# Last attention of a two-block transformer kernel: score matmuls of two heads issued in turn, and a fourth buffer for the position biases

## The reference

```python
proj = h @ w_in                                   # q, k, v of 3 groups x 16 heads, and a gate z
for g, (window, dilation) in enumerate(((128, 1), (512, 4), (2048, 16))):
    q, k = rms_norm(q_g), rms_norm(k_g)           # per head of 64
    logits = q @ k.T * 64 ** -0.5 + bias[distance, head]   # only causal distances that are
                                                  # multiples of dilation, up to window
    out_g, lse_g = softmax(logits) @ v, logsumexp(logits)
o = sum_g softmax_over_groups(lse)_g * out_g      # the same as one softmax over all keys of all groups
x = x + (o * silu(z)) @ w_out
```

## Time and profile before

| | us |
|---|---|
| median of 3 runs | 2271.77 (2268.54 to 2274.81) |
| profiled execution, its own time | 2273.13 |
| span of the profiled execution | 2271.3 |
| mean granted PE clock over the span | 0.884 |
| busy: PE / PEld / DVE / ACT / POOL | 2038.2 / 1693.6 / 1237.4 / 911.3 / 74.3 |

### The profile page before, as it was taken

One profiled execution on the slowest core, in us unless ns is written; L12 is line 12 of the kernel. 1 busy time (PEld: TensorE's weight loads), 2 busy tenths in 40 slices (PEclk: granted clock), 3 DMA queues, 4 the chain that ended last, 5 costly groups with the idle time before them and its releaser, 6 DMA issues.

```text
span 2271.3 us, 27874 instructions
## 1 busy us (share of the span) xinstructions
PE 2038.2 (90%) x11307; PEld 1693.6 (75%) x11307; DVE 1237.4 (54%) x1928; ACT 911.3 (40%) x1213; POOL 74.3 (3%) x135
## 2 busy tenths in 40 slices
PE   5899878868999999989967789987999899999998
PEld 3678656546777777868835668966999698888887
DVE  3553365653655565554356557765666554555443
ACT  4434512232444443344352245544334355664221
POOL 0100000011000000010000100001000000000000
PEclk8899977769999999989957799998999999997557
DMA  7534100002345442224300045544666455545321
GB/s 260 176 127 159 61 1 1 1 1 93 127 154 160 153 149 80 97 90 147 130 19 1 1 158 186 186 157 122 188 188 188 153 151 174 176 163 121 40 31 37
DMA packets 211453, 261.41 MB, mean 115 GB/s; under 512 B 4657, under 2 KB 173283, under 8 KB 211071
## 3 DMA queue, kind: packets, MB, share of 16 engines
q1 hardware_dynamic: 207690, 248.34, 33.8%
q0 software_dynamic: 3232, 11.15, 3.0%
q10 hardware_dynamic: 405, 0.15, 0.0%
HBM read 258.50 MB, written 1.12 MB: 114 GB/s over the span
## 4 chain that ended last, share of the span: by engine, by line
PE 68%; issue 13%; DVE 10%; ACT 4%; DMA 4%; POOL 1%; SPq 0%; DVEq 0%; ACTq 0%; POOLq 0%
PE acc L625 16%; PE acc L626 15%; PE acc L627 15%; PE acc L1068 3%; PE acc L1091 3%; DVE scratch L1784 2%; PE acc L799 2%; PE acc L655 2%; PE acc L656 2%; PE acc L1080 2%; ACT weights_high L1230 1%; DVE weights_low L1618 1%; PE acc L844 1%; PE acc L1024 1%; PE acc L847 1%
## 5 line engine op out<-in xcount | busy, mean ns | idle before, releaser
L1618 DVE TENSOR_TENSOR weights_low<-weights,weights_high 128x2048 fp32r<-128x2048 f32 x232 | 526.6, 2273 | 586.5 <-ACT weights_high L1230 586.2
L1230 ACT ACTIVATE weights_high<-weights 128x2048 fp32r<-128x2048 f32 x232 | 439.9, 1899 | 609.2 <-DMA weights<-in_w_ada_dram 117.2
L625 PE MATMUL acc<-normed_t_high,weights_high 128*128 128x256 f32 (+1 forms) x1824 | 577.5, 317 | 4.8 <-DVE normed_t_low L1652 2.6
L626 PE MATMUL acc<-normed_t_low,weights_high 128*128 128x256 f32 (+1 forms) x1824 | 564.8, 310 | 0.0
L627 PE MATMUL acc<-normed_t_high,weights_low 128*128 128x256 f32 (+1 forms) x1824 | 563.4, 309 | 0.0
L625 PEld LDWEIGHTS acc<-normed_t_high,weights_high 128*128 128x128 f32 x1824 | 346.4, 190 | 36.6 <-DVE normed_t_low L1652 6.8
L626 PEld LDWEIGHTS acc<-normed_t_low,weights_high 128*128 128x128 f32 x1824 | 343.9, 189 | 22.7 <-issue 3.8
L627 PEld LDWEIGHTS acc<-normed_t_high,weights_low 128*128 128x128 f32 x1824 | 344.1, 189 | 20.7
L625 PE MATMUL acc<-weights_high,normed_t_high 128*128 128x512 f32 (+1 forms) x792 | 314.0, 397 | 28.5 <-DVE normed_t_low L1925 28.4
L626 PE MATMUL acc<-weights_low,normed_t_high 128*128 128x512 f32 (+1 forms) x792 | 310.3, 392 | 0.0
L627 PE MATMUL acc<-weights_high,normed_t_low 128*128 128x512 f32 (+1 forms) x792 | 310.0, 391 | 0.0
(11 more groups left out here) (216 smaller groups left out, 2238.7 us busy)
## 6 DMA issues: line engine op xcount, KB each, us to landing
weights<-in_w_ada_dram SPq DMA_DIRECT2D x48, 1024.0 KB, 5.2
weights<-in_w_up_dram SPq DMA_DIRECT2D x44, 1024.0 KB, 6.4
weights<-in_attn_w_in_dram SPq DMA_DIRECT2D x40, 1024.0 KB, 5.1
weights<-in_conv_w_in_dram SPq DMA_DIRECT2D x32, 1024.0 KB, 5.8
weights<-in_w_in_dram SPq DMA_DIRECT2D x24, 1024.0 KB, 6.3
weights<-in_w_down_dram SPq DMA_DIRECT2D x20, 1024.0 KB, 5.0
weights<-in_w_out_dram SPq DMA_DIRECT2D x8, 1024.0 KB, 5.1
weights<-in_conv_w_out_dram SPq DMA_DIRECT2D x8, 1024.0 KB, 5.0
```

The source lines that it names most:

```text
L625: pe.matmul(o, ah, bh, start=start, stop=False)
L626: pe.matmul(o, ah, bl, start=False, stop=False)
L1230: act.activation(hi_slot(n)[:, 0:used], slot(n)[:, 0:used], ACT.Copy).then_inc(hi_in.sem, 1)
L1618: dve.tensor_tensor(slot(n, ring_lo)[:, 0:used], slot(n)[:, 0:used], hi_slot(n)[:, 0:used], ALU.subtract).then_inc(lo_in.sem, 1)
```

## The change

The list of units is reordered so that two neighbouring heads form a pair: (0,0), (1,0), (0,1), (1,1), (2,0), ... PE issues scores only in even steps, for the two units st and st+1 (same t, heads 2i and 2i+1), matmul by matmul in turn: group 0 of the even head, group 0 of the odd head, and so on, first all of the two first banks, then the two second banks. Transposes and V products keep their places, one unit per step. VectorE and ScalarE run the same loops as before, over the new list. The biases get a fourth buffer, in the space of `ht_b` (which the low part of the split input uses until the last gate product): head h goes to buffer h modulo 4, from head 4 on it waits for the maximum of unit (h-4, 1), and head 3 waits for the last of the gate products `z2`.

```diff
--- before.py
+++ after.py
@@ -225,7 +225,9 @@
         cosT, sinT = part(wide, 256), part(wide, 256)
         m0 = at[0]
         SM = part(wide, 2304).rearrange("p (d l n) -> p d l n", d=2, l=9)
-        BIAS = wide[:, m0:m0 + 2304].rearrange("p (b g n) -> p b g n", b=3, g=NG)
+        bias_old = wide[:, m0:m0 + 2304].rearrange("p (b g n) -> p b g n", b=3, g=NG)
+        BIAS = [*(bias_old[:, b, :, :] for b in range(3)), ht_b[:, 0:768].rearrange("p (g n) -> p g n", g=NG)]
+        NBIAS = len(BIAS)
         MASK = masks[:, :].rearrange("p (d l n) -> p d l n", d=2, l=LEVELS)
         pos = [0]
 
@@ -298,7 +300,7 @@
         s_fw = sem("final_weight_in")
         s_vec = sem("bias_rows_out")
         s_hot = sem("hot_in")
-        s_bias = [sem(f"bias_in{i}") for i in range(3)]
+        s_bias = [sem(f"bias_in{i}") for i in range(NBIAS)]
         s_out = sem("result_out")
         vector_step, scalar_step, pool_step = sem("vector_step"), sem("scalar_step"), sem("pool_step")
 
@@ -369,7 +371,7 @@
         q_rs = S("qk_scale", QKEYS)
         q_done = S("qk_scaled", QKEYS)
         zk = [(c, t) for c in range(2) for t in range(2)]
-        BU = [(h, t) for h in range(NH) for t in range(2)]
+        BU = [(2 * i + j, t) for i in range(NH // 2) for t in range(2) for j in range(2)]
         b_max = S("b_max", BU)
         b_exp = S("b_exp", BU)
 
@@ -1058,16 +1060,19 @@
                         pe.wait_ge(*taken_after(("v2", g, c, t)))
             U = len(BU)
             for st in range(U + 3):
-                if st < U:
-                    h, t = BU[st]
-                    r = slice(64 * (h % 2), 64 * (h % 2) + 64)
+                if st < U and st % 2 == 0:
+                    t = BU[st][1]
                     n = (t + 1) * P
                     for part_, gs in enumerate(((0, 1), (2,))):
-                        o = open_group(("s2", st, part_))
+                        outs = [open_group(("s2", u, part_)) for u in (st, st + 1)]
                         for g in gs:
-                            last = pe.matmul(o[:, g % 2 * 256:g % 2 * 256 + n], QK2[r, g, 0, h // 2, cols_of(t)],
-                                             QK2[r, g, 1, h // 2, 0:n], start=True, stop=True)
-                        last.then_inc(full, 1)
+                            for u, o in zip((st, st + 1), outs):
+                                h = BU[u][0]
+                                r = slice(64 * (h % 2), 64 * (h % 2) + 64)
+                                last = pe.matmul(o[:, g % 2 * 256:g % 2 * 256 + n], QK2[r, g, 0, h // 2, cols_of(t)],
+                                                 QK2[r, g, 1, h // 2, 0:n], start=True, stop=True)
+                                if g == gs[-1]:
+                                    last.then_inc(full, 1)
                 if 0 <= st - 2 < U:
                     u = st - 2
                     h, t = BU[u]
@@ -1196,12 +1201,14 @@
 
 
             for h in range(NH):
-                if h >= 3:
-                    pool.wait_ge(b_max.sem, b_max.after((h - 3, 1)))
+                if h >= NBIAS:
+                    pool.wait_ge(b_max.sem, b_max.after((h - NBIAS, 1)))
+                elif h == 3:
+                    pool.wait_ge(full, full_after(("z2", 3)))
                 src = bass.AP(tensor=vec_d.tensor, offset=h * 384, ap=[[1, P], [NH * 384, NG], [1, 256]])
-                pool.dma_start(BIAS[:, h % 3, :, :], src).then_inc(s_bias[h % 3], 16)
-            for b in range(3):
-                pool.wait_ge(s_bias[b], 16 * len(range(b, NH, 3)))
+                pool.dma_start(BIAS[h % NBIAS], src).then_inc(s_bias[h % NBIAS], 16)
+            for b in range(NBIAS):
+                pool.wait_ge(s_bias[b], 16 * len(range(b, NH, NBIAS)))
 
 
         @block.scalar
@@ -2098,7 +2105,7 @@
                     b = u % 3
                     n = (t + 1) * P
                     if t == 0:
-                        dve.wait_ge(s_bias[h % 3], 16 * (h // 3 + 1))
+                        dve.wait_ge(s_bias[h % NBIAS], 16 * (h // NBIAS + 1))
                     if u >= 3:
                         dve.wait_ge(full, full_after(("eT", u - 3, 1)))
                     for part_, gs in enumerate(((0, 1), (2,))):
@@ -2107,7 +2114,7 @@
                         g0, ng = gs[0], len(gs)
                         src = bank(key).rearrange("p (g n) -> p g n", g=2)[:, 0:ng, 0:n]
                         dve.scalar_tensor_tensor(LG[:, b, g0:g0 + ng, 0:n], src, 0.125,
-                                                           BIAS[:, h % 3, g0:g0 + ng, 256 - n:256], ALU.mult, ALU.add).then_inc(taken_of(key), 1)
+                                                           BIAS[h % NBIAS][:, g0:g0 + ng, 256 - n:256], ALU.mult, ALU.add).then_inc(taken_of(key), 1)
                         dve.wait_ge(*taken_after(key))
                     dve.tensor_reduce(bred[:, b:b + 1], LG[:, b, :, 0:n], AX.XY, ALU.max).then_inc(vector_step, line.one())
                     dve.wait_ge(vector_step, line.n)
```

## The result

The changed kernel takes 2210.58 us (median of 4 runs, 2207.61 to 2214.21) against 2270.15 us beside it: ratio 0.9742, 95% interval 0.9718 to 0.9766. The profiled execution took 2207.61 us, with a span of 2205.7 us against 2271.3. In that pair of profiles the last attention ran from 2069.54 to 2235.39 us before and from 2069.09 to 2169.32 us after: 65.6 us, the whole difference of the spans.

What follows compares the result with a forecast made beforehand. PE's instruction stream at clock 0.50 was taken as the bound. Start 1.6, six pairs at 3.84 and end 3.3 gave 27.9 us; with 7.6 for the clock 35.5, so 2236 us, range 2214 to 2253.

Steps and rivals of the forecast that it cites:

- Bound before: Last attention: PE's own instruction stream is the one bound, busy 159.83 of 159.90 us at clock 0.50.
- Scores in pairs: Last attention: two heads' scores in opposite row halves overlap fully, saving 4.44 us per pair of heads.
- S1: The t=1 scores of a pair of heads, forecast at 2.86 us instead of 5.72 at the lower level.
- S0: The t=0 scores of a pair of heads, forecast at 1.58 us instead of 3.16 at the lower level.
- Order and waits: Per pair, PE waits 0.6 us for VectorE's bias addition before the t=0 V product; 16.9 us per pair, 3.84 saved.
- sign of being wrong: The prediction would be wrong if, among other signs, PE waits over 2 us per pair.
- Ends of the stage: Last attention: 1.6 us saved at the start, 3.3 us in the last pair and drain.
- Fourth buffer: Bias transfers: worth 0 by itself, guards against a wait of up to a microsecond or so.
- The clock: Last attention: the level lifts after four of eight S1 and drops again, 1.9 us each, 7.6 us saved.
- rival 2: The level stays up through most of the last attention, VectorE bounds, 11.2 us per pair: 2204 us, chance 0.14.

Runs made afterwards that it cites:

- e6: The changed kernel with only the t=1 scores issued in pairs, t=0 scores one unit per step: 2241.34 us, ratio 0.9867.
- e3: The changed kernel with each score bank's matmuls issued head after head instead of in turn: 2211.87 us, ratio 0.9746.
- e4: The changed kernel with both heads of a pair in the same row half, so nothing can overlap: 2260.52 us, ratio 0.9959.
- e8: The changed kernel with ScalarE's copy of the transposes ahead of its exponential: 2203.36 us, ratio 0.9714.
- f4: f2 with full-array 512-column filler matmuls in PE's waits at the start of the stage: 2214.35 us, ratio 0.9734.
- e1: The kernel before with the fourth bias buffer alone: 2265.77 us, ratio 0.9992.
- e2: The changed kernel with three bias buffers instead of four: 2220.55 us, ratio 0.9781.
- e5: The changed kernel with only the t=0 scores issued in pairs, t=1 scores one unit per step: 2205.89 us, ratio 0.9720.
- g3: e4 with a full-array filler matmul of 256 columns ahead of each unit's scores: three runs 2218.70, 2234.33, 2249.21 us, ratio 0.9834.
- g4: The changed kernel with a full-array filler matmul of 256 columns ahead of each unit's scores: 2222.68 us, ratio 0.9782.
- e7: The kernel before with an added full-array matmul of 512 columns ahead of each unit's scores: 2232.46 us, ratio 0.9842.
- f3: The kernel before with an added full-array matmul of 256 columns ahead of each unit's scores: 2228.74 us, ratio 0.9815.
- f1: The changed kernel with a 512-column full-array filler before the even head's t=0 V product: 2204.40 us, ratio 0.9698.
- f2: The changed kernel with only t=0 scores paired and ScalarE's copy ahead of its exponential: 2210.94 us, ratio 0.9731.

## Why the prediction was wrong

- *Bound before:* right. PE, at the lower level, always busy.
- *Scores in pairs, 4.44 us per pair at the lower level:* right as to size. S1 2.86 us (e6, in turn) and 2.87 (e3) against 2.86 forecast, S0 1.59 in the changed kernel (2080.68 to 2082.27) against 1.58. But the saving per pair was priced at the lower level, which held for a quarter of the stage only; at the upper level VectorE's chain takes most of it back.
- *Order and waits:* the place was right (the t=0 V product behind S1), the size depends on the level. At the lower level e4 shows 0.41 us there against 0.6 forecast, without overlap; at the upper it is 1.32. ScalarE's copy was held covered; at the upper level it ends last, but only 0.17 us behind VectorE (1.15 in e8). PE's waits come to 2.1 to 2.2 us per pair, over the 2 us that the prediction named as a sign of being wrong.
- *Ends of the stage:* the start is mostly VectorE's (f4), right, but only 0.6 us were saved there, not 1.6. The end saved 10.0 us instead of 3.3, at the upper level.
- *Fourth buffer:* nothing by itself (e1), right. With the pairs it keeps off waits of up to 1.3 us for a transfer (e2), as forecast; what that is worth in the total is open.
- *The clock:* this step failed. "Between none and one per pair I take four: 7.6 us." It treated each lift as a short one that ends by itself, as in the earlier trace rows. The level stays up for 20 to 30 us at a time, three quarters of the stage, and PE's work then takes 11.2 to 11.4 us per pair instead of the 16.9 forecast. The mechanism was there as rival 2, with the right 11.2 us and 2204 us for the kernel, but with a chance of 0.14 and mostly left out of the range. The weighing was wrong. Against rival 2 the prediction set that PE would wait a third of the time and that the level falls after such stretches; at the upper level PE waits a fifth of the time, and the level mostly doesn't fall. In the upper windows of the earlier trace rows PE was busy 2.28 and 1.20 of 3.20 us. Whether that difference is the reason is not shown.
- The trigger was named wrongly too: S1's overlap alone lifts briefly (e6), that of the t=0 pairs alone lifts and holds (e5).

How the 60 us divide: with the level up, the overlap is worth some 7 us (g3 against g4, 0.9 us per pair). With the level down it is worth 28 us by the forecast; e6, with the t=1 half alone and five short lifts, took 26.5. The level without the overlap is worth 35 to 43 us with fillers in the way (e7, f3). They don't add: the overlap pays either in PE time at 1.2 GHz or by lifting the level to 2.4, after which PE waits for VectorE.

Open: why the level falls in one pair and not in the next. Neither PE's waits nor its busy share sort the profiles. The change waits 1.32 us in each pair and fell behind two of these waits; f1 still waits 1.15 us and didn't fall. Before its fall f2 was busy 24.75 of 27.10 us (91%), f1 without a fall 70.25 of 83.10 (85%). e3, with the change's own order of steps, had two falls of 10 us, at 2108.0 and 2145.6.

## What to carry to other kernels

When a stage is PE-bound at 0.50 of the clock while always busy, look at how much of the array its matmuls fill, and price the upper level for the whole stage, bounded by the next engine, as a main case: fuller work can hold the level, not only touch it. Matmuls that contract over 64 rows can be issued for two row halves near each other in different banks; strict turns aren't needed. A useless full-array matmul in the stream is a cheap test of what the level is worth before anything is rewritten.

## What the runs showed of the hardware

- Added full-array work made a PE-bound stage faster: 32 matmuls of 256 columns, 2228.74 against 2272.00 us, the level at 1.00 from 2075.0 to 2181.2 instead of 0.50 (f3).
- PE can be busy for 159.83 of 159.90 us and stay at 0.50.
- Matmuls of two row halves run together even when queued four and four: S1 in 2.87 us for twelve records (e3).
- The Trainium skill ("TensorE: Matmul & The Clock Gate", PE-mode transpose) says that transposes don't count as busy for the clock. In the changed kernel the first lift, at 2083.4, comes behind S0 and six transposes (2080.68 to 2083.4). The V products and S0 before them may have been enough, so this doesn't test the rule; no run took the transposes alone. Once the level is up, they do run at it: three take 0.38 us in the change (2111.24 to 2111.62) and 0.69 at 0.50.
